# Up projection of a gated MLP by Strassen's seven products per a/b tile pair, in a split-precision float32 kernel

## What is computed

```python
x = x + merged @ w_out
ffn_out = conv_ffn(rmsnorm(x, g_ffn), conv_buf, w_up, w_dw, b_dw, w_down)
x = x + ffn_out
x = x + (p_i @ w_ple) * jax.nn.sigmoid(rmsnorm(x, g_ple) @ w_ple_gate)

def conv_ffn(h, buf, w_up, w_dw, b_dw, w_down):      # h (L, 1024), w_up (1024, 2 * 2816)
    a, b = jnp.split(h @ w_up, 2, axis=-1)
    full = jnp.concatenate([buf, a], axis=1)
    conv = b_dw + sum(full[:, t:t + L] * w_dw[t] for t in range(3))
    y = (jax.nn.gelu(conv) * b) @ w_down
```

## Time and profile before

| | |
|---|---|
| median of 3 runs | 1628.82 us (1628.69 to 1630.73) |
| the profiled execution's own time | 1629.12 us |
| its span, first to last instruction | 1627.1 us |
| PE busy | 1576.9 us (97%), 10088 matmuls |
| PEld busy | 1533.3 us (94%), 10088 loads |
| DVE, ACT, POOL busy | 752.5, 327.8, 558.2 us |
| TensorE's granted clock, mean | 0.99 |
| DMA | 91.1 MB, mean 56 GB/s |

### The profile page before, as it was taken

The page is one execution under the profiler, slowest core; times in us unless marked ns, Lnnn a source line. Parts: engine busy times, 40 slices in busy tenths (PEclk is TensorE's granted clock), DMA queues, the critical chain, the costliest instruction groups (busy, mean ns, idle before and its releaser), DMA issues.

```text
span 1627.1 us, 23324 instructions
## 1 busy us (share of the span) xinstructions
PE 1576.9 (97%) x10088; PEld 1533.3 (94%) x10088; DVE 752.5 (46%) x956; ACT 327.8 (20%) x541; POOL 558.2 (34%) x282
## 2 busy tenths in 40 slices
PE   7999999999999999999999999999999999999992
PEld 7988888889999999989999999999999999999992
DVE  7665444433231154455434444343344534467555
ACT  5025444443000021122110101001010100113211
POOL 2331311223343433334343433433333434343330
PEclk9999999999999999999999999999999999999996
DMA  6410211101111132121111111111111111111102
GB/s 236 132 37 15 83 69 40 34 27 46 46 40 52 39 111 87 52 66 39 52 39 53 39 52 39 52 40 53 39 52 39 45 47 52 40 44 49 39 14 107
DMA packets 27879, 91.11 MB, mean 56 GB/s; under 512 B 4472, under 2 KB 4480, under 8 KB 27656
## 3 DMA queue, kind: packets, MB, share of 16 engines
q1 hardware_dynamic: 24904, 79.86, 15.7%
q10 hardware_dynamic: 2880, 9.84, 1.6%
HBM read 83.00 MB, written 9.83 MB: 57 GB/s over the span
## 4 chain that ended last, share of the span: by engine, by line
PE 93%; DVE 3%; issue 2%; DMA 1%; ACT 1%; SPq 0%; DVEq 0%
PE ps L524 73%; PE ps L536 4%; PE ps L538 4%; PE ps L537 4%; PE ps L659 2%; PE ps L681 2%; PE ps L633 2%; DMA x_in<-xT 1%; DVE acc L1082 1%; DVE x_res L1448 1%; DVE h_lo L1022 1%; DVE rms L1114 0%; DVE rms L1037 0%; PE ps L601 0%; DVE acc L1031 0%
## 5 line engine op out<-in xcount | busy, mean ns | idle before, releaser
L493 POOL TENSOR_TENSOR w_hi<-w_raw,zero 128x1024 fp32r<-128x1024 f32 x122 | 230.8, 1892 | 1006.6 <-PE ps L524 734.0
L524 PE MATMUL ps<-h_hi,w_hi 128*128 128x352 f32 x1536 | 332.8, 325 | 6.5 <-DVE gap L1036 2.9
L524 PE MATMUL ps<-h_hi,w_lo 128*128 128x352 f32 x1536 | 331.0, 323 | 0.0
L524 PE MATMUL ps<-h_lo,w_hi 128*128 128x352 f32 x1536 | 330.7, 323 | 0.0
L495 POOL TENSOR_TENSOR w_lo<-w_raw,w_hi 128x1024 fp32r<-128x1024 f32 x122 | 325.5, 2668 | 9.6
L524 PEld LDWEIGHTS ps<-h_hi,w_hi 128*128 128x128 f32 x1536 | 261.2, 189 | 9.4 <-issue 9.4
L524 PEld LDWEIGHTS ps<-h_hi,w_lo 128*128 128x128 f32 x1536 | 263.8, 188 | 0.0
L524 PEld LDWEIGHTS ps<-h_lo,w_hi 128*128 128x128 f32 x1536 | 260.8, 188 | 0.0
L1332 DVE TENSOR_TENSOR x_res<-ps,x_res 128x1056 f32<-128x1056 f32 x96 | 120.6, 1256 | 148.2 <-PE ps L524 148.2
L536 PE MATMUL ps<-h_hi,w_hi 128*128 128x352 f32 x480 | 160.3, 334 | 10.1 <-DVE w_lo L1064 8.7
L538 PE MATMUL ps<-h_hi,w_lo 128*128 128x352 f32 x480 | 155.1, 323 | 0.0
(11 more groups left out here) (169 smaller groups left out, 1726.0 us busy)
## 6 DMA issues: line engine op xcount, KB each, us to landing
w_raw<-w_stream SPq DMA_DIRECT2D x124, 512.0 KB, 3.6
x_in<-xT SPq DMA_DIRECT2D x8, 528.0 KB, 9.1
x_res<-xT ACTq DMA_DIRECT2D x8, 528.0 KB, 6.6
o_y<-x_res ACTq DMA_DIRECT2D x8, 528.0 KB, 2.9
bias_lines<-bias_line SPq DMA_DIRECT2D x1, 3072.0 KB
bias_sb<-bias_lines SPq DMA_DIRECT2D x4, 640.0 KB, 5.1
o_v<-vT SPq DMA_DIRECT2D x4, 272.0 KB, 2.1
o_k<-kT SPq DMA_DIRECT2D x4, 272.0 KB, 2.5
```

Source lines behind the costliest of these rows:

```text
L493: pool.tensor_tensor(w_hi[k][:], w_raw[k][:], zero[:].broadcast_to([P, KT * P]), ALU.add).then_inc(w_hi_done, 1)
L524: mm = pe.matmul(out[:, c, :], w, x[:, c * CW:(c + 1) * CW], start=first and n == 0, stop=last and n == 2)
```

## The change

Each a/b tile pair of the up projection is computed as a 2 x 2 block product. The activations are cut in a left and a right half of 528 frames (HT) and an upper and a lower half of 512 input channels (HK = 4 blocks); the weights in a and b, upper and lower half. Strassen's scheme gives the pair by seven products instead of eight, each of 4 * 3 matmuls on 2 chunks of 264 frames (HW), so 24 matmuls; products 4 and 5 are accumulated onto the banks of products 0 and 1. Seven sums or parts of the activations (`op_hi`, `op_lo`) are made once: five during the output projection, two (`late_op`) while the first products run. Seven sums or parts of the weights are made for every pair: five additions on GpSimd (`piece_add`), seven roundings on ScalarE (`pieces_upto`), seven subtractions on GpSimd (`piece_low`), in a ring of four pieces of 128 x 512. SP loads half tiles into four halves of the raw buffers. The outputs a and b are put together from PSUM by ScalarE (`copy_first`, `copy_second`) and VectorE (`read_3` to `read_4`), and scaled by 1/rms from SBUF (`scale_a`, `scale_b`).

The order is a list of frames, U for a pair and D for a down projection: U0 U1 | U2 D0 U3 | U4 D1 U5 | ... | U18 D8 U19 | U20 U21 D9 D10. What follows a pair (conv, GELU, mid) is done in the next frame, as `pending`. The down projection uses one bank per unit: 24 units (8 output blocks x 3 chunks) of 6 matmuls of 352 columns, over 8 banks. The weights behind the MLP are split only when its last matmul is done.

```diff
+REGIONS = (2, 1, 0, 3, 2, 1, 0)
+for _g in range(1, GROUPS - 1):
+    FRAMES += [("U", 2 * _g), ("D", _g - 1), ("U", 2 * _g + 1)]
+FRAMES += [("U", FT - 2), ("U", FT - 1), ("D", GROUPS - 2), ("D", GROUPS - 1)]
...
         @block.gpsimd
+            def slot_free(q):
...
+                    pool.wait_ge(ffn_done, piece_event(q - 4))
...
+            for n, fr in enumerate(FRAME):
+                q = fr.piece
+                if fr.kind == "U":
+                    piece_add(n, fr, 1, 1, 2, ALU.add)
+                    piece_low(q, half_raw(1))
+                    piece_add(n, fr, 2, 1, 3, ALU.add)
+                    piece_low(q + 1)
+                    piece_add(n, fr, 3, 0, 3, ALU.add)
+                    piece_low(q + 2)
+                    piece_add(n, fr, 4, 1, 0, ALU.subtract)
+                    piece_low(q + 3)
+                    piece_add(n, fr, 5, 3, 2, ALU.subtract)
+                    piece_low(q + 4)
+                    piece_low(q + 5)
+                    piece_low(q + 6, half_raw(3))
+                else:
+                    for i, h in enumerate(HALVES):
+                        piece_low(q + i, half_raw(h))
+            pool.wait_ge(ffn_done, EVENTS)
+            for s in range(S_FFN, STREAM):
+                split(s, s // 2, s % 2, tile_done, s - 1 - S_JOB)
...
         @block.tensor
+            def up(f, i, ready=None):
...
+                pe.wait_ge(piece_split, q + 1)
...
+                if i == 6:
+                    pe.wait_ge(ffn_copied, 3 * f + 2)
+                elif free_product(fr, i) > 0:
+                    pe.wait_ge(ffn_read, free_product(fr, i))
+                for b in range(HK):
...
+                    for n, (w, x) in enumerate(((w_h, op_hi), (w_h, op_lo), (w_l, op_hi))):
+                        for c in range(2):
+                            mm = pe.matmul(region(i, c), w[:, col], x[i][:, b, c * HW:(c + 1) * HW],
+                                           start=b == 0 and n == 0 and i not in (4, 5),
+                                           stop=b == HK - 1 and n == 2, skip_group_check=i in (4, 5))
...
         @block.scalar
+            for fr in FRAME[1:]:
+                if pending is not None:
+                    pieces_upto(fr.piece + 3)
+                    ffn_conv0(pending)
+                    pieces_upto(fr.piece + 4)
+                    ffn_gelu(pending)
+                    pieces_upto(fr.piece + 5)
+                    ffn_mid_hi(pending)
+                    pending = None
+                if fr.kind == "U":
+                    pieces_upto(fr.piece + 5)
+                    copy_first(fr.n)
+                    pieces_upto(fr.piece + 6)
+                    copy_second(fr.n)
+                pieces_upto(fr.piece + fr.pieces)
...
         @block.vector
+            def scale_b(f):
+                own(f, 7)
+                dve.tensor_tensor(b_row[f % 2][:], b_row[f % 2][:], rms[:], ALU.mult).then_inc(b_ready, 1)
...
+            read_3(0)
+            late_op(0)
+            read_5(0)
+            late_op(1)
+            late_op(2)
+            read_2(0)
+            late_op(3)
+            read_3_6(0)
+            invert2(0)
+            invert2(1)
+            read_5_7(0)
+            invert2(2)
+            read_4(0)
...
+            def up_frame(f, pending):
+                if pending is not None:
+                    ffn_conv(pending)
+                read_3(f)
+                read_5(f)
+                if pending is not None:
+                    ffn_mid(pending)
+                    ffn_lo(pending)
+                read_2(f)
+                read_3_6(f)
+                read_5_7(f)
+                read_4(f)
+                scale_a(f)
+                scale_b(f)
```

More of the change, by code:

```diff
@@ L746, in _ @@
                     branches(step)
[L749 to L756, removed]
@@ L759, in up @@
[L759 to L763, removed]
-                pe.wait_ge(mid_split, 2 * g + 2)
[L766 to L782, removed]
+            for k in range(KT):
+                tile_ready(S_OUT + k)
+                product((J_OUT + k, J_OUT + k - 1), k % 2, m_hi, m_lo, ready=(m_split, 1) if k == 0 else None
+                        ).then_inc(tile_done, 1)
@@ new lines, in norm2, with down @@
+            def norm2(c, out):
+                pe.wait_ge(acc_done, 2 * (KT - 1))
+                pe.matmul(out, ones[:], acc[:, c * CW:(c + 1) * CW], start=True, stop=True).then_inc(norm_done, 1)
+            def down(g):
+                fr = DOWN[g]
+                pe.wait_ge(mid_split, 2 * g + 2)
+                for u in range(UNITS):
+                    m, c = u // CH, u % CH
+                    q = fr.piece + m // 2
+                    if u % (2 * CH) == 0:
+                        pe.wait_ge(piece_split, q + 1)
+                    pe.wait_ge(ffn_read, free_unit(fr, u))
+                    for b in range(2):
+                        col = slice((2 * (m % 2) + b) * P, (2 * (m % 2) + b + 1) * P)
+                        x_h, x_l = (x[mid_slot(2 * g + b)][:, c * CW:(c + 1) * CW] for x in (mid_hi, mid_lo))
+                        pe.matmul(unit_bank(u), piece_hi(q)[:, col], x_h, start=b == 0, stop=False)
+                        pe.matmul(unit_bank(u), piece_hi(q)[:, col], x_l, start=False, stop=False)
+                        mm = pe.matmul(unit_bank(u), piece_lo(q)[:, col], x_h, start=False, stop=b == 1)
+                    mm.then_inc(ffn_done, 1)
@@ new lines, in _ @@
+            up(0, 0, ready=(3, 5))
+            up(0, 1, ready=(4, 5))
+            up(0, 2, ready=(5, 5))
+            up(0, 3)
+            pe.wait_ge(ffn_copied, 2)
+            norm2(0, bank(0, CW))
+            norm2(1, bank(1, CW))
+            up(0, 4)
+            pe.wait_ge(ffn_read, 3)
+            norm2(2, bank(6, CW))
+            up(0, 5, ready=(22, 2))
+            pe.wait_ge(root_done, 5)
+            up(0, 6, ready=(21, 2))
+            pe.wait_ge(root_done, 6)
+            for fr in FRAME[1:]:
+                if fr.kind == "U":
+                    for i in range(PRODUCTS):
+                        up(fr.n, i)
+                else:
+                    down(fr.n)
@@ L979, in ffn_tile, with ffn_mid_hi @@
+            def ffn_mid_hi(f):
                 act.wait_ge(mid_ready, f + 1)
[L980 to L988 removed]
@@ L997, in _ @@
                 square(x_res[:, k, :], 2 * KT + k)
[L998 removed]
+            root(7, J_NORM3, J_NORM3)
             for k in range(KT):
@@ new lines, in up_done, with own, copied, of_right @@
+            def up_done(f, i):
+                dve.wait_ge(ffn_done, UP[f].event + i + 1)
+            def own(f, n):
+                dve.wait_ge(ffn_read, UP[f].read + n)
+            def copied(f, n):
+                dve.wait_ge(ffn_copied, 3 * f + n)
+            a_left = halves(a_row[:, 2:2 + HT])
+            rest = SEQ - HT - HW
+            a_right = [a_row[:, 2 + HT:2 + HT + HW], a_row[:, 2 + HT + HW:2 + SEQ], a_row[:, SAMPLE_A:AW]]
+            def of_right(x):
+                return [x[:, 0, :], x[:, 1, 0:rest], x[:, 1, rest:HW]]
@@ new lines, in _, with low_p @@
+            late_op(3)
[5 more added lines that the diff above has]
+            read_4(0)
+            dve.wait_ge(rms_ready, 2 * CH)
+            scale_a(0)
+            scale_b(0)
+            def low_p():
+                for k in range(2):
+                    dve.wait_ge(p_hi_done, k + 1)
+                    dve.tensor_tensor(p_lo[:, k, :], p_raw[:, k, :], p_hi[:, k, :].bitcast(F32), ALU.subtract
+                                      ).then_inc(p_split, 1)
@@ L1384, in down_ready @@
+            pending = 0
+            for fr in FRAME[1:]:
+                if fr.kind == "U":
+                    up_frame(fr.n, pending)
+                    pending = fr.n
+                else:
+                    down_frame(fr.n, pending)
+                    pending = None
             def down_ready(m, s, parts):
```

497 lines of the change are left out of this document (377 added, 120 removed).

## The result

| | before | after |
|---|---|---|
| median of 7 runs each, same chip | 1629.14 us (1628.65 to 1631.47) | 1637.43 us (1634.29 to 1638.66) |
| ratio, 95% interval | | 1.0041 [1.0029, 1.0052] |
| profiled execution | 1629.12 us, span 1627.1 | 1638.66 us, span 1636.9 |
| TensorE's granted clock, mean | 0.990 | 0.977 |

The changed kernel is 0.4% slower. 1619 us were forecast: the time is in the range, the sign is the wrong one. The seven runs after lie in two groups, three from 1634.29 to 1634.69 us and four from 1637.43 to 1638.66; the profile is of the slowest, no trace of the faster group exists, and why there are two stays open.

What follows compares the result with a forecast made beforehand. TensorE's matmuls were taken to bound the kernel, provided the work feeding them stays hidden. 1629.1 - 56.4 (matmuls) + 37 (stalls) + 6 (first pair) + 3.5 (behind the MLP) gave 1619 us, range 1582 to 1648.

Steps and rivals of the forecast that it cites:

- Term 1: MLP up-projection matmuls: 3696 of 264 columns at 0.1235 us instead of 3168 at 0.1619, a gain of 56.4 us.
- Rivals 3 and 4: Matmul distance: 2.4 GHz rule or 0.11 us, 1588 us (chance 0.10); or columns don't set it, 1724 us (0.05).
- Term 2: Twelve frames U following a frame U: lock-slowed chain makes product 4 late, 3.05 us each, 37 us in all.
- `mid` to 13.7: Frame U after U: `mid` gets the lock before GpSimd's piece 4 subtraction, which ends at 14.9; product 4 3.0 us late.
- no further loss: Frame U after U: piece 5 is ready at 17.8, just when product 5 is due; 0 us added.
- rival 2: Frames U after U: every VectorE lock falls behind a GpSimd instruction, 5.3 us late each, 1646 us; chance 0.23.
- Rival 1: Frames U after U: locks fall between the steps and no frame stalls, 1582 us; chance 0.20.
- Term 3: First pair: last operand block, late operands and reciprocals cost 8.9 us, less 2.9 stood before: +6, from 3 to 12.
- Term 4: Behind the MLP: the `w_ple` split waits for the last matmul, some 5.3 us; net +3.5, from 2 to 6.
- the 45 us named: MLP in the profile after: TensorE's idle sum would be about 45 us.

Runs made afterwards that it cites:

- the last experiments: Kernel with pieces 4 and 5 rounded ahead of the GELU, plus piece 6 rounded early, weight buffers swapped behind the MLP, `scale_b` just before `mid`: 1577.81 us.
- the second experiment: Changed kernel with ScalarE's roundings of pieces 4 and 5 moved ahead of the GELU in frames U: 1600.50 us, ratio 0.9819.

## Why the prediction was wrong

**Term 1 was right.** 122.3 ns a matmul where 123.5 was taken, a frame of 20.54 us for 20.75. The reading in proportion to the columns (121.4) is the nearer one. With the frames D, 2.3 us shorter where nothing was expected, the gain is 63.2 for 56.4. Rivals 3 and 4 fall by the distance.

**Term 2 is where it went wrong**, 59.3 us for 37. Place, releaser and mechanism were right in the main: twelve frames, idle ahead of product 4, released by L670 (though another 0.4 to 2.0 us stand ahead of product 5). So were the steps up to `mid`: in U6 `scale_a` ends at 4.0 (forecast 4.1), `scale_b` at 6.3 (6.3), the convolutions at 8.5 and 10.8 (8.6 and 10.8). The step that failed is "`mid` to 13.7. The subtraction of piece 4 waits for it and ends at 14.9". The forecast itself had `mid` ask at 12.4 and the subtraction ready at 12.6; measured, the subtraction begins at 12.6 and the large part of `mid` 0.08 us behind it. So product 4 was less late than forecast (13.9 for 14.9), and piece 5, "to 17.8", is there at 19.0. The frame is 24.97 for 23.8. Against 20.54 that is 4.43 each, 53.2 in twelve; another 6.1 are in U1, U2, U14 and U21, and 4.6 of these are the clock: in U2, U14 and U21 the last 48 matmuls took 7.64 us for 6.12. Of the two ways to be late rival 2 had the right idea (`mid` behind a GpSimd instruction), with one more lock than there is.

**A second step failed beneath it,** "product 5 is due at 14.9 + 2.96 = 17.8: no further loss". It takes the clock at 1.00 behind a stall of 3 us. The wait that enforced the forecast's order shows what it is worth: 1644.7 us. With the order as forecast, one frame in twelve (U21, 24.15 us) came near the 23.8. In the changed kernel the fallen clock in product 4 is hidden by the wait for piece 5; it becomes visible wherever something shortens that wait, by 1.55 us a frame. Rival 1, that no frame stalls, is wrong for this order, but the reordered kernel of the last experiments comes to it: 1577.8 us.

**Term 3**: 7.1 us net for 6: 12.2 in the first frame (of the 8.9 forecast, 5.5 were in it and 3.4 in U1, which is only 0.5 us longer than the steady ones), less 5.0 where 2.9 was taken. It was split otherwise than forecast: 3.3 for the last block (3.5 forecast), and 2.5 at the norm behind product 3, where the late operands' roundings keep ScalarE from its copies. And the clock, at nothing in this term, fell twice in the frame: its mean was 0.58 from 703 to 707 us, where product 1 took 4.44 us for 2.93, and 0.57 from 717 to 721.

**Term 4**: 4.6 for 3.5. The stall was 5.6 us as worked out (5.3); the half clock lasted longer than before, from 1478.4 to 1485.2 (1.3 us of it while TensorE still stood) against 1477.6 to 1481.0:

```profile
1480.00:1485.00 5.00, 5.00 (x18) 5.00 (x18) 0.52 (x1) 0.00 (x0) 4.64 (x2) 0.50 0.35 108
```

Not in the sum at all are 1.9 us: the first matmul of the output projection starts at 603.27 instead of 601.34, behind parts that the change leaves as they were. Nothing shows it to be a cost of the change: in the runs of the experiments, whose code up to there is that of the changed kernel, this matmul starts anywhere from 600.35 to 603.13. Frames U behind a D and frames D stall nowhere, as forecast, and TensorE's idle time in the MLP is near the 45 us named (37.6 + 3.3 + 2.5 + 0.8).

**The sum of it:** 22.3 us in term 2, 1.1 in term 3, 1.1 in term 4 and 1.9 at the start, less 6.8 in term 1, is 19.6, and 1638.7 - 1619 is 19.7. Strassen's products do give their 61 us. The kernel gives most of them back because ScalarE's order makes weight pieces, which are ready, queue behind a pair's GELU and `mid`, which are not: of the 59.3 us of stalls in term 2, moving two roundings gave 37 back.

## What to carry to other kernels

When an engine serves two chains, write its queue so that nothing that is ready stands behind something that waits: two roundings moved ahead of the GELU were worth 37 us, and with a third one, `scale_b` later and another buffer the same program does 1577.8 us, 3.1% under the kernel before. A stall is followed to the last piece that is late, not to the wait that the profile names first: freeing product 4 alone gained nothing. And where two engines meet at a lock within 0.2 us of each other in a forecast, as here, it should carry both orders, and price the clock behind each stall.

## What was not expected of the hardware

- TensorE's clock fell to its lower level inside a dense stream: for about 3.4 us behind stalls of 1.9 to 2.8 us (two matmuls 0.44 us apart for 0.245), behind stalls of 3.4 us for as long in some frames and until 5.8 us past the restart in others, and until 5.5 us past the restart behind the stall of 5.6 us. In the steady frames of the second experiment, with gaps of 0.8 us, it stayed at 1.00. Behind the same stall it fell in one frame (10.60 us for 72 matmuls) and not in another (9.05).
- A stall that is taken away can give back more than itself, and one that is shortened less: when `scale_b` was cut, the chain got 1.8 us shorter in eleven frames, some 20 in all, and 11 came.
- 352-column float32r matmuls are 160.4 ns apart in the frames D of the changed kernel, one bank a unit, and 161.9 in the kernel before, three banks in turn. No run tells whether the banks are the reason.
